# Transposes and ScalarE sums for the modulation, a two-pass rotary key group, and another order at the first plain pair

## The reference, cut to what matters

```python
mod = silu(c) @ w_ada + b_ada                  # 1024 -> 6144, per stream
sh1, sc1, g1, sh2, sc2, g2 = split(mod, 6)
h = rms_norm(x, norm_mix_g) * (1 + sc1) + sh1
c_q, c_kv, k_r, u, g_b, g_c = split(h @ w_in)  # 768, 256, 32, 512, 512, 512
latent = rms_norm(c_kv, kv_norm_g)
k_rope = apply_rope(k_r, pos)
y_conv = g_b * conv(g_c * u)                   # three taps
mix = concat([attention(...), y_conv]) @ w_out
x = x + g1 * mix
h = rms_norm(x, norm_ffn_g) * (1 + sc2) + sh2
ff = (silu(h @ w_gate) * (h @ w_up)) @ w_down  # 2816 wide
x = x + g2 * ff
y = rms_norm(x, final_norm_g)
```

## Time and profile before

| | us |
|---|---|
| median of three runs | 1406.61 (1405.75 to 1407.39) |
| the profiled execution | 1405.67 |
| its span, first to last instruction | 1403.3 |
| TensorE busy | 1369.1 (98%) |
| VectorE busy | 906.2 (65%) |
| ScalarE busy | 436.3 (31%) |
| mean granted clock of TensorE | 0.996 |

### The profile page before, as it was taken

One profiled execution on the slowest core, in us unless ns is written; L12 is line 12 of the kernel. 1 busy time (PEld: TensorE's weight loads), 2 busy tenths in 40 slices (PEclk: granted clock), 3 DMA queues, 4 the chain that ended last, 5 costly groups with the idle time before them and its releaser, 6 DMA issues.

```text
span 1403.3 us, 23871 instructions
## 1 busy us (share of the span) xinstructions
PE 1369.1 (98%) x9660; PEld 1289.3 (92%) x9660; DVE 906.2 (65%) x1445; ACT 436.3 (31%) x705; POOL 46.6 (3%) x40
## 2 busy tenths in 40 slices
PE   7999999999999999999999999999999999999997
PEld 4599999999998676689999999999999999999996
DVE  7789778364564467778775565656556555656566
ACT  4521110124401444345642323223232323232223
POOL 0000000000003122100000000000000000000000
PEclk9999999999999999999999999999999999999999
DMA  9344444611213322030210212021111112111103
GB/s 371 101 135 135 135 136 106 250 36 48 88 19 68 112 74 43 1 107 1 61 35 28 74 45 60 30 60 30 60 45 44 60 30 75 45 58 32 60 30 124
DMA packets 112950, 107.11 MB, mean 76 GB/s; under 512 B 9552, under 2 KB 97192, under 8 KB 112128
## 3 DMA queue, kind: packets, MB, share of 16 engines
q1 hardware_dynamic: 110288, 105.09, 24.6%
q10 hardware_dynamic: 2608, 1.28, 0.3%
HBM read 88.93 MB, written 9.88 MB: 70 GB/s over the span
## 4 chain that ended last, share of the span: by engine, by line
PE 90%; DVE 5%; ACT 2%; DMA 1%; SPq 1%; issue 1%; POOL 0%; DVEq 0%; POOLq 0%
PE PS L1166 29%; PE PS L763 18%; PE PS L1184 17%; PE PS L1076 4%; PE PS L930 4%; PE PS L1056 3%; PE PS L1288 3%; PE PS L1114 2%; PE PS L1267 1%; PE PS L1003 1%; PE PS L862 1%; DMA ADA<-in_w_ada 1%; PE PS L816 1%; PE PS L1023 1%; PE PS L958 1%
## 5 line engine op out<-in xcount | busy, mean ns | idle before, releaser
L2284 DVE TENSOR_TENSOR EL<-HALF_W,EH 128x512 fp32r<-128x512 f32 x163 | 112.1, 688 | 122.8 <-ACT EH L1591 121.8
L1591 ACT ACTIVATE EH<-HALF_W 128x512 fp32r<-128x512 f32 x163 | 102.2, 627 | 256.8 <-PE PS L1184 151.3
L2420 DVE SCALAR_TENSOR_TENSOR X<-PS,MOD,X 128x792 f32<-128x792 f32 (+2 forms) x240 | 125.3, 577 | 70.3 <-PE PS L1184 70.3
L1166 PE MATMUL PS<-HBL_T,EH 128*128 128x264 f32 x640 | 169.7, 285 | 0.0
L1166 PE MATMUL PS<-HBH_T,EH 128*128 128x264 f32 x640 | 169.4, 285 | 0.0
L1184 PE MATMUL PS<-AL,EH 128*128 128x264 f32 x640 | 162.7, 285 | 0.0
L1184 PE MATMUL PS<-AH,EH 128*128 128x264 f32 x640 | 162.3, 284 | 0.0
L763 PE MATMUL PS<-HH,WH 128*128 128x352 f32 x456 | 148.2, 326 | 0.5 <-DVE WL L1871 0.5
L763 PE MATMUL PS<-HL,WH 128*128 128x352 f32 x456 | 146.7, 322 | 0.0
L1166 PE MATMUL PS<-HBH_T,EL 128*128 128x264 f32 x640 | 130.1, 284 | 0.0
L1166 PE MATMUL PS<-HBL_B,EH 128*128 128x264 f32 x480 | 127.2, 285 | 0.0
(11 more groups left out here) (315 smaller groups left out, 2834.7 us busy)
## 6 DMA issues: line engine op xcount, KB each, us to landing
ADA<-in_w_ada SPq DMA_DIRECT2D x22, 1024.0 KB, 5.4
HALF_W<-in_w_gate SPq DMA_DIRECT2D x22, 512.0 KB, 3.7
HALF_W<-in_w_up SPq DMA_DIRECT2D x22, 512.0 KB, 3.9
HALF_W<-in_w_down SPq DMA_DIRECT2D x22, 512.0 KB, 3.8
RAW<-in_w_in SPq DMA_DIRECT2D x20, 512.0 KB, 6.3
x_saved_rows<-X SPq DMA_DIRECT2D x2, 2112.0 KB, 12.3
X<-x_saved_rows SPq DMA_DIRECT2D x4, 1056.0 KB, 6.6
out<-ORW SPq DMA_DIRECT2D x8, 512.0 KB, 2.6
```

Source lines behind the costliest of these rows:

```text
L1166: mm = pe.matmul(PS[:, 2 * s + n, 0:HQ], w, x[:, k, n * HQ:(n + 1) * HQ], start=(first and w is wh and x is xh), stop=(ends and w is wl), ...
L1591: act.activation(dst if len(src.shape) == 2 else dst.rearrange("p (k c) -> p k c", k=2), src, ACT.Copy)\
L2284: dve.tensor_tensor(el, src, eh.bitcast(F32), ALU.subtract).then_inc(entry_lo, 1)
L2420: ins = dve.scalar_tensor_tensor(dst, src, MOD[:, G2 + m, st:st + 1], dst, ALU.mult, ALU.add)
```

## The change

Five edits, in the order of the diff.

1. `ada` makes four transposes (the pieces of ACC against IDENT) into bank 6 or 7, by turns, instead of four products with ONES. ScalarE's new `sum_ada(n)` waits for it and copies each 128 x 128 result onto itself with an accumulated sum per row, into a column of a new small tile MRAW. `ada(n)` from n = 2 on waits until the sums of n - 2 are made. `add_bias` reads MRAW and waits for `ada_summed`.
2. TensorE's loops over convolution and output groups and ScalarE's over the convolution groups are written out; the `ada` keep their places.
3. The rotary key group's weights lie side by side: ScalarE rounds the 64 used columns to columns 0 to 63, VectorE writes the rest to columns 64 to 127. TensorE multiplies these 128 columns with the rounded and the rest part of the operand: 8 x 3 x 2 = 48 matmuls. Rows 0 to 63 are the part by the rounded weights, rows 64 to 127 that by the rest. ScalarE copies rows 64 to 127 out, VectorE adds rows 0 to 63, and that addition frees the banks.
4. At the first plain pair, the totals of the second half stand ahead of the last step of product 0 instead of behind it, and the spread ahead of the fourth step of product 1 instead of the fifth. ScalarE rounds entries 0 and 1 two tiles earlier, and entry 4 behind the first SiLU; VectorE makes the rests of entries 0 and 1 behind the additions of tiles 5 and 6.
5. The semaphore of the last transposes is `rows_turned`, with its nine earlier counts added.

```diff
-            def ada(n, bank, col, dyn=0):
-
-                pe.wait_ge(acc_ready, 2 * dyn + (2 * n + 6))
+            def ada(n):
+
+                pe.wait_ge(acc_ready, 2 * n + 6)
+                if n >= 2:
+                    pe.wait_ge(ada_summed, n - 1)
                 for m in range(2):
                     for st in range(2):
-                        mm = pe.matmul(PS[:, bank, bass.ds(col + (2 * m + st), 1)],
-                                       ACC[:, n % 2, st, m * P:(m + 1) * P], ONES[:, 0:1], start=True, stop=True)
+                        q = 2 * m + st
+                        mm = pe.transpose(PS[:, 6 + n % 2, q * P:(q + 1) * P], ACC[:, n % 2, st, m * P:(m + 1) * P],
+                                          IDENT[:])
                 mm.then_inc(ada_used, 1)
...
+            begin_slot(S_KR)
+            begin_group(G_KR)
+            wk = weights_of(S_KR)[0]
+            for k in range(KD):
+                for n in range(NCH):
+                    for x in h:
+                        mm = pe.matmul(PS[:, NCH * (G_KR % 2) + n, 0:CH], wk[k], x[k][:, n * CH:(n + 1) * CH],
+                                       start=(k == 0 and x is h[0]), stop=(k == KD - 1 and x is h[1]))
+            mm.then_inc(ps_full[G_KR % 2], 1)
...
-                    if n == 1 and b == 1:
-                        half_spread(1, 3)
                     for k in range(KH):
+                        if (n, b, k) == (0, 1, KH - 1):
+                            half_totals(1, 21)
+                        if (n, b, k) == (1, 0, KH - 1):
+                            half_spread(1, 3)
                         if q == 0:
                             pe.wait_ge(operand_lo, KD * t + KH * b + k + 1)
                         first_step(n, b, k)
-                if n == 0:
-                    half_totals(1, 21)
...
+            def sum_ada(n):
+
+                act.wait_ge(ada_used, n + 3)
+                for q in range(4):
+                    turned_tile = PS[:, 6 + n % 2, q * P:(q + 1) * P]
+                    ins = act.activation(turned_tile, turned_tile, ACT.Copy, accum_out=MRAW[:, 4 * n + q:4 * n + q + 1])
+                ins.then_inc(ada_summed, 1)
+
+            for i in range(2):
                 for n in range(6):
...
                     keep(G_CONV + n, (UU[:, 0:T], CC[:], BB[:])[q], 3 * i)
+                    for a in ADA_USED[i][n]:
+                        sum_ada(6 * i + a)
             for n in range(1, 4):
                 split_hi(S_COUT + n + 1, G_COUT + 2 * n - 1)
+                sum_ada(n + 11)
+            sum_ada(15)
...
-            act.activation(in_chunks(CQ[0:64, KQ - 1, :]), chunks(G_KR, slice(0, 64)), ACT.Copy)\
-                .then_inc(ps_free[G_KR % 2], 1)
+            act.activation(in_chunks(CQ[0:KRW, KQ - 1, :]), chunks(G_KR, slice(KRW, P)), ACT.Copy)\
+                .then_inc(k_rope_part, 1)
...
-                if m >= 6:
-                    round_first(m - 6)
+                if m in (4, 5):
+                    round_first(m - 4)
...
-            round_first(4)
             act.wait_ge(summed, 21)
             silu_first(0, 0)
+            round_first(4)
...
-            dve.wait_ge(ada_used, 14)
-            add_bias(7, 16, 24, 2)
+            dve.wait_ge(ada_summed, 12)
+            add_bias(MRAW[:, 0:48], 16, 24, 2)
...
-            dve.wait_ge(ada_used, 18)
-            add_bias(6, 40, 8, 3)
+            dve.wait_ge(ada_summed, 16)
+            add_bias(MRAW[:, 48:64], 40, 8, 3)
...
+            dve.wait_ge(k_rope_part, 1)
+            dve.tensor_tensor(in_chunks(CQ[0:KRW, KQ - 1, :]), in_chunks(CQ[0:KRW, KQ - 1, :]),
+                              chunks(g, slice(0, KRW)), ALU.add).then_inc(ps_free[g % 2], 1)
             wait_kept(dve, g)
...
+                if m in (5, 6):
+                    rest_early(m - 5)
                 for q in ((), (), (0,), (1, 2), (3, 4), (5, 6), (7,), ())[m]:
                     rest_first(q)
-                if m == 6:
-                    rest_early(0)
...
-            for q in range(1, 4):
+            for q in range(2, 4):
                 rest_early(q)
```

More of the change, by code:

```diff
@@ L42 @@
 CHUNK = 64
+KRW = 64
 EPS = 1e-6
@@ L112 @@
 ADA_BANK = (4, 5, 7, 3)
+ADA_USED = (((), (), (0,), (1, 2), (3,), (4, 5)), ((), (0, 1), (2,), (), (3, 4), (5,)))
 def x_load(u):
@@ L156, in build @@
         o = 8 * U + 24576
+        MRAW = at("MRAW", [P, 4 * 16], F32, ARENA - 256)
         COS = at("COS", [P, T], F32, o)
@@ L305, in build @@
         ada_used = sem("ada_used")
+        ada_summed = sem("ada_summed")
         mod_kept = sem("mod_kept")
@@ L878, in conv_group @@
                 for a in used:
-                    ada(a, 7, 24 * i + 4 * a, 6 * i)
-            ada(0, 7, 0)
+                    ada(6 * i + a)
+            ada(0)
             for n in range(2, 6):
[L883 to L886, removed]
+                conv_group(n, ADA_USED[0][n] if n > 2 else ())
+            for n in range(6):
+                conv_group(n, ADA_USED[1][n], 1)
             y = cut((YH, YL))
[L888 to L897, removed]
+            for n in range(4):
+                begin_slot(S_COUT + n)
+                for m in range(2):
+                    g = G_COUT + 2 * n + m
+                    begin_group(g)
+                    product(g, weights_of(S_COUT + n, NJ, m), y, range(NJ),
+                            before=(lambda k: pe.wait_ge(y_lo, k + 2)) if n + m == 0 else None)
+                ada(n + 12)
+            for n in range(KKV):
                 begin_slot(S_CKV + n)
@@ L1242, in turn @@
                                       X[:, m, u * P:u * P + r], IDENT[:])
-                mm.then_inc(y_turned, 1)
+                mm.then_inc(rows_turned, 1)
             def last_down():
@@ L1419, in _ @@
                     act.wait_ge(kr_half_loaded, 16)
-                split_hi(S_CKV + n + 1, G_CKV + n - 1)
+                    wait_loaded(act, S_KR)
+                    wait_filled(act, G_CKV + n - 1)
+                    act.activation(hi_lo(S_KR)[0][:, :, 0:KRW], raw(S_KR)[:, :, 0:KRW], ACT.Copy)\
+                        .then_inc(w_hi, 1)
+                else:
+                    split_hi(S_CKV + n + 1, G_CKV + n - 1)
                 keep(G_CKV + n, CKV[:, n, :])
@@ L1829, in invert, with add_bias @@
                 dve.wait_ge(rstd_ready, n + 1)
-            def add_bias(bank, first, n, done):
-                src = PS[:, bank, 0:2 * n].rearrange("p (m s) -> p m s", s=2)
+            def add_bias(sums, first, n, done):
+                src = sums.rearrange("p (m s) -> p m s", s=2)
                 for st in range(2):
@@ L1888, in _ @@
             dve.wait_ge(ada_turned, 4)
-            add_bias(6, 0, 16, 1)
+            add_bias(PS[:, 6, 0:32], 0, 16, 1)
             scales(A1, SC1, V_NMIX)
@@ L1986, in _ @@
                     add_gated(G_COUT + 2 * n + m, G1, 2 * n + m)
-            dve.wait_ge(ada_used, 18)
-            add_bias(6, 40, 8, 3)
+            dve.wait_ge(ada_summed, 16)
+            add_bias(MRAW[:, 48:64], 40, 8, 3)
             dve.memset(KR[0:64, :], 0.0).then_inc(zeroed, 1)
             dve.memset(SSQ[:], 0.0).then_inc(zeroed, 1)
-            for n in range(KKV):
-                split_lo(S_CKV + n + 1)
+            split_lo(S_CKV + 1)
+            dve.wait_ge(w_hi, S_KR + 1)
+            kr = hi_lo(S_KR)[0]
+            dve.tensor_tensor(kr[:, :, KRW:P], raw(S_KR)[:, :, 0:KRW], kr[:, :, 0:KRW].bitcast(F32), ALU.subtract)\
+                .then_inc(w_lo, 1)
             split_lo(S_KR + 1)
@@ L2009, in _ @@
             ins.then_inc(k_rope_part, 1)
-            dve.wait_ge(k_rope_part, 1)
+            dve.wait_ge(k_rope_part, 2)
             for rows, op in ((lo, ALU.subtract), (up, ALU.add)):
```

4 lines of the change are left out of this document (1 added, 3 removed).

## The result

| | before | after |
|---|---|---|
| median, measured together | 1406.18 (1405.38 to 1407.39, 4 runs) | 1392.75 (1391.55 to 1393.84, 4 runs) |
| ratio, 95% interval | | 0.9898 [0.9886, 0.9911] |
| profiled execution | 1405.67 | 1391.83 |
| its span | 1403.3 | 1390.0 |

The changed kernel is 1.0% faster. The forecast was 1395.1 with a range from 1393.0: the sign and the three mechanisms hold, and the size is missed by 2.35 us, 0.25 us beyond the end of the range. In what follows, two disturbed executions are left out, one of e11 (1653.26 us) and one of the kernel before beside e9 to e12 (6846.13 us). Most lines moved in the code: L745, L763, L862, L1123, L1131 and L1288 are now L751, L769, L868, L1137, L1145 and L1302.

A forecast was written before the change was run, and what follows sets the result against it. TensorE was taken as the bound, with 90% of the chain. Terms of 6.0, 2.6 and 2.9 us sum to 11.5; 1405.67 less that is 1394.2, plus 0.94 to the median 1395.1 us, range 1393.0 to 1399.4.

The forecast's parts named there:

- the three mechanisms: Cheaper modulation sums, fewer rotary key matmuls and an earlier first plain pair: 6.0, 2.6 and 2.9 us.
- Modulation: Each `ada`: four transposes replace eight matmul instructions, saving 0.38 us per single and 0.84 per pair, 6.0 us in all.
- number 11: The single `ada` before the first output group: saves nothing, because TensorE waits for YL anyway, until 209.68.
- Rotary key: Rotary key group: 48 matmuls instead of 72 save 3.9 us, VectorE's added operation costs 1.3, net 2.6 us.
- F + 15.2: F is the end of the rotary group's matmuls; rotary chain and second query group's weights come 15.2 us later.
- First plain pair: Start of the feed-forward part: pair starts 2.7 us earlier, totals wait about 0.1 us; gain taken as 2.9 us.
- rival (d): TensorE's clock falls behind the transposes, 1.4 us lost at each of twelve places: slower, 1412 us; chance 0.03.
- those bounds: Low and high sums of the three terms, 7.3 and 12.1 us, giving 1394.5 to 1399.3 us.
- rival (e): More than forecast: the added operation and the break at a transpose cost less, 1393.0 us; chance 0.07.
- (a): First plain pair: its gain stays out because late squares make TensorE wait at the totals, 1398.0 us; chance 0.08.
- (b): Convolution part: VectorE becomes the bound and the 6.0 us become idle time, 1401.1 us; chance 0.05.
- (c): Modulation sums: transposes cost their duration of 0.27 us, not their spacing, 1404.8 us, no change; chance 0.03.

The follow-up runs named there:

- e11: Changed kernel with ScalarE's sums of each modulation row made twice (64 more copies and reads): 1392.45 us, only 3 runs.
- e9: Changed kernel with 18 filler transposes in the opening, and ScalarE rounding the second query group's weights ahead of the root: 1391.01 us.
- e12: Kernel before with only TensorE's and ScalarE's loops written out: 1406.67 us against 1406.62.
- e1: Kernel before, unchanged, measured again: 1405.97 us (1404.25 to 1409.19).
- e3: Kernel before with 18 transposes of IDENT in TensorE's wait for a load in the opening: 1405.51 us (1403.46 to 1408.48).
- e8: Kernel before with 18 transposes in the opening's wait and 20 in the pause ahead of the first plain pair: 1404.13 us against 1406.22.
- e5: Kernel before with the modulation's edits alone (edits 1, 2 and 5): 1399.97 us against 1406.22.
- e6: Kernel before with the two-pass rotary key group alone (edit 3): 1402.85 us against 1406.22.
- e7: Kernel before with the new order at the first plain pair alone (edit 4): 1402.30 us against 1406.22.
- e2: Changed kernel, unchanged, measured again: 1392.89 us (1392.19 to 1394.77), ratio 0.9909 to the kernel before.
- e4: Changed kernel with 18 transposes of IDENT in TensorE's wait for a load in the opening: 1391.65 us, 4 runs.
- e10: Changed kernel with each modulation sum's four transposes made twice, 64 transposes more: 1399.59 us, 5 runs.

## Why the prediction was nearly right, and where it failed

All fourteen profiled executions can be made comparable by two rows of the chain. The start of the first `ada` tells how much the opening lost, to the clock and to a load that landed later (the earliest is 76.59), and the first product at the pair whether the clock fell there (6.1 us, or 7.6, +1.5). Taking both from the span:

| kernel | span | first `ada` starts | first product | span less both |
|---|---|---|---|---|
| before | 1403.3 | 78.25 | 6.09 | 1401.6 |
| e1 before | 1405.7 | 79.00 | 7.61 | 1401.8 |
| e12 loops | 1404.0 | 77.10 | 7.60 | 1402.0 |
| e3 before filled | 1401.7 | 76.59 | 6.11 | 1401.7 |
| e8 both filled | 1402.4 | 77.03 | 6.16 | 1402.0 |
| e5 modulation | 1398.2 | 77.94 | 7.58 | 1395.4 |
| e6 rotary | 1399.4 | 76.98 | 6.10 | 1399.0 |
| e7 order | 1400.5 | 78.38 | no pause | 1398.7 |
| after | 1390.0 | 76.72 | no pause | 1389.9 |
| e2 after | 1393.0 | 79.66 | no pause | 1389.9 |
| e4 after filled | 1389.9 | 76.73 | no pause | 1389.8 |
| e9 | 1389.1 | 76.59 | no pause | 1389.1 |
| e10 | 1397.8 | 78.46 | no pause | 1395.9 |
| e11 | 1390.4 | 76.93 | no pause | 1390.1 |

Spans of 1401.7 to 1405.7 come down to 1401.6 to 1402.0, and 1389.9 to 1393.0 to 1389.8 to 1389.9. The five kernels without the change have a mean of 1401.8, so the edits are worth 11.9 us, and alone the modulation 6.4, the rotary key 2.8, the order 3.1 (terms: 11.5, 6.0, 2.6, 2.9).

- **Modulation, right.** Four transposes at 0.45 us and eight at 0.87 were taken from eight in a row elsewhere; found were 0.44 and 0.87. From the first `ada`'s start on to the first latent group the chain is 6.2 us shorter (78.25 to 255.39 before, 76.72 to 247.69 after). No wait for the sums appeared, and number 11 saved nothing, as worked out: TensorE waits 1.0 us for YL where it waited 0.45. The 29 us put down for ScalarE's sums were too many (16 x 1.2 = 19), which cost the forecast nothing.
- **Rotary key, right.** 48 matmuls take 7.70 us instead of 11.69, and the added operation 1.25 where 1.26 was taken. The second query group starts 15.15 us behind the end of the rotary group (278.58 to 293.73), the prediction's F + 15.2; before it was 13.87. The first query group starts at F + 2.59 where F + 2.55 was worked out. It had been F + 1.33, so it comes 1.26 later, and this is the "wait of about 1.2"; the 0.83 of the waits is the same delay, counted from the end of the last matmul. 0.7 follow at WL; e9 takes the second wait away, and its profiled span is 0.8 shorter than e4's.
- **First plain pair, right.** The pause of 2.7 us is gone, the totals wait 0.43 us where 0.1 was worked out, and the chain of scaling is no longer last. 702.54 against 715.78 behind the last of these products is 13.24 us earlier, of which 10.25 stood ahead of the pair: 3.0.
- **The step that failed** is the last line of the sum, "1405.67 - 11.5 = 1394.2, and with the 0.94 us to the median 1395.1 us". It carries the clock of one execution over to the median of another kernel. The 2.35 us between forecast and median are, in the two profiled executions (13.84 us apart): 0.3 of the terms by the milestones, 1.5 because before's execution lost 1.66 us in the opening by chance and after's 0.13, and 0.5 outside the span (2.37 against 1.83). The median that the prediction had for before (1406.61) lies 0.94 above its execution, and after's lies 0.92 above its own, so the offset cancelled, and the chance remained. The term for the clock was nothing; the runs show 1.5 us of it in this pair of executions.
- **A mechanism was missing, too.** By medians the change is worth 13.1 to 13.4 us, not 11.9, and a part of the rest is that the clock fell behind the pause ahead of the pair in three of the six profiled executions that have it (e1, e5, e12 against before, e3, e6), at 1.5 us each time, and in none of the eight in which the pause was gone or filled. The three were measured on three different chips, so it isn't one chip's. That is 0.75 us on the mean, and e8 puts it at 1.2 by the median spans. The prediction had seen this pause and argued the reverse from a single row: rival (d)'s "after the idle of 2.72 us at 662 the clock stayed at 1.00". One execution shows what can happen, not how often. For the runs it allowed "up to a microsecond to either side", which a fall of 1.5 us exceeds. The range itself, 1393.0 to 1399.4, isn't those bounds (1394.5 to 1399.3) with a microsecond on either side; its lower end is rival (e)'s time.
- **Rivals.** (a) and (b) didn't come: e7 keeps the pair's gain, e5 that of the modulation. (c) fell with e10. (d), that the clock falls behind the transposes, is contradicted where it was thought likeliest: the four and eight in a row are followed by 11.59 us groups throughout, and in after the granted clock is 1.00 from 100 to 112 us, from 125 to 148 and from 212 to 223. (e), more than forecast, was nearest, for another reason than its own: the added operation took 1.25 us, and the break at a transpose is as worked out.

Left open: what decides whether the clock falls in an execution. From 25 to 50 us it fell in six of ten profiled executions without the filler (all but after, e6, e10 and e11), with it in none of four; that is suggestive and no more, and in before the filler moved the median by only 0.5 us. From 50 to 60 us it fell in twelve of fourteen, three of the four filled ones among them (all but after and e4). Of the difference of medians, 0.5 to 0.8 us lie beyond 11.9 and the pair's 0.75. About 0.4 of them stand outside the span: what the time has beyond the span is 2.2 us in the mean of before's 23 runs beside e2, and 1.8 in e2. It is 1.8 in e3, e8 and e12 as well and 2.5 in e10, so it doesn't go by the change; what sets it is not known.

## What to carry to other kernels

Ahead of a sum, bring the baseline to a known clock: compare the start of an early step and one product behind each pause over several executions, and write the forecast against that, not against one. A pause of TensorE of 2.7 us cost half as much again behind it (1.5 us), in part of the executions; so removing one can be worth more than its length, and filling it with work of no use can win that extra back and narrow the spread. What has a row in a similar place (eight transposes between matmuls, a product out of PSUM of the same width) can be priced to some hundredths of a microsecond.

## What the hardware showed that was not expected

- The clock fell behind an idle time of 2.7 us in some executions and not in others (before and e1 are the same program), and the work behind took 7.6 us in place of 6.1. Twenty transposes of a constant into a free bank in that pause kept it at 1.00 (one profiled execution, and a range of 1.8 us over 11 runs where e3's 12 have 5.0).
- The Trainium skill, in "TensorE: Matmul & The Clock Gate", section "Part 4: PE-mode transpose", says that transposes don't count as busy for the clock gate in the same way. With fillers made of nothing else (e3, e4, e8, e9) the clock was 1.00 from 25 to 50 us in all four profiled executions, and behind the filled pause of e8. So here they seem to count, or to help in some other way; that is not shown, as a filler of plain matmuls was not tried, and four executions could also have kept the clock by chance.
- A copy of 128 x 128 in PSUM onto itself with a running total, and the read of it, follow each other every 0.285 us on ScalarE, though their durations are 0.26 and 0.18.
- An `ada` of four fp32 products with a single column took 0.78 to 0.83 us, nearly twice what four transposes of 128 columns take (0.44): each product is two instructions of 0.10 us.
